# First, second and last RMS norm of a two-block transformer kernel: squares by parts, normalisation by halves or chunks, and a reciprocal in two halves

## Chip, cores and metric

The kernel runs on one core of one Trainium2 chip. The metric is the device time of one execution in microseconds. Of the kernel before, three runs were timed; one more execution was taken by the profiler.

## What is computed

Two blocks on x of 256 tokens by 2048 features, all float32. The rows that matter here:

```python
def rmsnorm(x, w):
    xf = x.astype(jnp.float32)
    xf = xf * lax.rsqrt(jnp.mean(xf * xf, axis=-1, keepdims=True) + EPS)
    return (xf * w.astype(jnp.float32)).astype(x.dtype)

# first_block
h = rmsnorm(x, ln1_w)                     # first norm
proj = h @ w_in                           # z, xbc, dt, q, k, v, f
y_ssd = ssd_group(...)                    # scan; its output is normalised in two groups of 512 features
y_fox = fox_group(...)                    # 16 heads of attention with a forget gate
x = x + jnp.concatenate([y_ssd, y_fox], axis=-1) @ w_out
x = x + peer(rmsnorm(x, ln2_w), ...)      # second norm, then 16384 experts
x = rmsnorm(x, lnf_w)

# second_block: conformer convolution and attention, cross attention, then
nm = rmsnorm_2(h, g_mlp[l])
h = h + jnp.square(jax.nn.relu(nm @ w1[l])) @ w2[l]
return rmsnorm_2(h, g_final)              # last norm
```

## The kernel before

**Weights as a stream.** All large weights lie in one stream of units of 128x2048 float32 (1 MB). SyncE loads them into four buffers (`raw`), and loads a buffer again when the unit in it has been split (`split_done`). Each unit is split into two float32r parts. ScalarE copies it (`hi`, tile w_hi), VectorE subtracts the copy from the original (`lo`, tile w_lo). `ahead(u)` on either engine does this for unit u+2 once TensorE has finished unit u (w_hi and w_lo have two buffers each). TensorE multiplies high by high, high by low and low by high: `feature_unit` does 48 matmuls of 256 columns for a unit, `row_unit` 24 of 512 columns.

**Tiles turned.** A matmul wants the activations with features on partitions. `turn_tile` transposes one of 16 feature tiles (two TensorE transposes) into one of four banks; ScalarE (`scaled_tile`) copies it with the norm's weight as scale into the high part of the tile a_both, VectorE (`scaled_lo`) computes the low part. TensorE may take a bank again when the low part of the tile four before it is written (`tmp_split`).

**Norms.** ScalarE's `square` squares a half of x (128 tokens by 2048) and sums into stat; GpSimd's `rsqrt` takes mean, epsilon and the power -0.5 (`rs_done`); VectorE's `normalise` multiplies both halves of x by it (`normed`). What stands around the three norms:

- First norm. ScalarE: two squares, casts of units 0 and 1, the high part of the small dt weights (wdtf to wd), 16 scaled tiles. VectorE: differences of units 0 and 1, `normalise`, the low part of wd, 16 low parts. TensorE: 16 tiles turned, 48 small matmuls for dt, their copy and two transposes, then 12 units of xbc. GpSimd issues the four small loads (consts, cols, rows, wdtf); all that need any of them wait for all of them (`s_small` 64).
- Second norm. The last out1 units end in `add_chunk`, in which VectorE adds 128x512 for each half of the tokens to x. After the last one come `squares`, the root, `normalise`, 16 tiles turned, and only then the first wq unit.
- Last norm. The same after the last down3 unit, with the norm's weight (`wide`) in VectorE's operation. SyncE then writes out each half of the tokens as it is ready (`fin`).

**The reciprocal.** In step 25 of 38 steps, in which v1, z, q, k and the first out1 units run beside the scan and the attention, VectorE takes the reciprocal of 128x512 root values (`rms`). Steps 25 to 28 scale two of eight tiles each with it and split them. Behind this stand in every step `head_max` (row maxima of one attention head's scores), `head_norm` of the head before, `out_split` in every second step, and `ahead`. TensorE may write the next head's scores only after `head_max` (one bank).

The order on each engine is the program's own, written out by hand; engines meet at semaphores only.

```python
if s == 25:
    eng.wait_ge(rt_done, 2)
    own.do(eng.reciprocal(rms[:, :, :], rms[:, :, :]))
if 25 <= s < 29:
    for i in (2 * (s - 25), 2 * (s - 25) + 1):
```

## Time and profile before

| what | us |
|---|---|
| median of three runs | 3184.81 |
| lowest, highest run | 3183.85, 3185.7 |
| profiled execution, device time | 3187.75 |
| its span, first to last instruction | 3185.9 |
| TensorE busy in the span | 3067.4 |
| VectorE busy | 2237.3 |
| ScalarE busy | 1400.6 |
| GpSimd busy | 143.3 |

The span is that of the profiled execution; the 1.85 us around it lie ahead of the first and behind the last instruction. Busy times of engines overlap. The mean granted clock of TensorE over the span is 0.989 of full speed (2.4 GHz; the lower level is 1.2 GHz).

### The profile page before, as it was taken

The numbers are of one execution on the slowest core, as the hardware profiler recorded it, in microseconds if no ns is written. First come the engines' busy times: TensorE is split into PE (matmuls) and PEld (weight loads), VectorE is DVE, ScalarE is ACT, GpSimd is POOL, SyncE is SP. The second block draws the span as 40 slices with busy tenths as digits, with TensorE's granted clock in tenths as the row PEclk, the third lists the DMA queues.
The fourth block names the chain that finished last, engine by engine and source line by source line (L and its number), as shares of the span: only waits on it lengthen the run. The fifth ranks groups of instructions, "written<-read, shape, count | busy, mean of one in ns | idle before, by whom it ended". The sixth has DMA issues, their size and how long they took to land.

```text
span 3185.9 us, 49641 instructions
## 1 busy us (share of the span) xinstructions
PE 3067.4 (96%) x19428; PEld 2810.2 (88%) x19428; DVE 2237.3 (70%) x3255; ACT 1400.6 (44%) x1640; POOL 143.3 (4%) x168
## 2 busy tenths in 40 slices
PE   6999989999999999999999999999898999999997
PEld 6898879899999999999999999998787888888886
DVE  4666548999867888888888677687655646555564
ACT  3465443356444444444444445334444333333332
POOL 1000000000101101010101000000000000000000
PEclk9999999999999999999999999999999999999999
DMA  4433454456767888888888664544343555555553
GB/s 186 178 141 131 146 197 148 170 189 235 244 245 279 314 300 311 298 310 300 308 298 312 239 238 172 186 166 152 130 174 107 197 190 189 188 188 194 186 188 126
DMA packets 95548, 673.14 MB, mean 211 GB/s; under 512 B 11528, under 2 KB 11552, under 8 KB 15424
## 3 DMA queue, kind: packets, MB, share of 16 engines
q1 hardware_dynamic: 77184, 562.07, 48.9%
q0 software_dynamic: 16224, 94.72, 8.8%
q10 hardware_dynamic: 2016, 14.68, 1.2%
q8 instruction: 80, 1.31, 0.2%
q14 instruction: 44, 0.36, 0.0%
HBM read 652.48 MB, written 18.89 MB: 211 GB/s over the span
## 4 chain that ended last, share of the span: by engine, by line
PE 85%; DVE 11%; ACT 2%; issue 1%; DMA 0%; DVEq 0%; SPq 0%; POOL 0%; POOLq 0%; ACTq 0%
PE bank L1768 29%; PE bank L1769 15%; PE bank L1796 6%; PE bank L1798 6%; PE bank L1797 6%; PE bank L1746 6%; PE bank L1748 5%; PE bank L1747 5%; DVE w_lo L1033 4%; PE bank L1774 2%; DVE pick_a L1429 1%; ACT w_hi L631 1%; DVE pick_b L1424 1%; PE bank L1860 1%; PE bank L1824 1%
## 5 line engine op out<-in xcount | busy, mean ns | idle before, releaser
L1033 DVE TENSOR_TENSOR w_lo<-raw,w_hi 128x2048 fp32r<-128x2048 f32 x532 | 1218.3, 2290 | 570.1 <-ACT w_hi L631 548.1
L1768 PE MATMUL bank<-a_both,w_hi 128*128 128x448 f32 (+1 forms) x3840 | 1258.3, 380 | 6.9 <-DVE a_both L1050 3.9
L1769 PE MATMUL bank<-a_both,w_lo 128*128 128x224 f32 (+1 forms) x4096 | 1060.5, 269 | 0.0
L1768 PEld LDWEIGHTS bank<-a_both,w_hi 128*128 128x128 f32 x3840 | 721.4, 188 | 90.3 <-DVE a_both L1050 4.4
L1769 PEld LDWEIGHTS bank<-a_both,w_lo 128*128 128x128 f32 x4096 | 778.2, 190 | 11.6
L631 ACT ACTIVATE w_hi<-raw 128x2048 fp32r<-128x2048 f32 x308 | 588.4, 1911 | 409.3 <-PE bank L1798 399.7
L1746 PE MATMUL bank<-a_both,w_hi 128*128 128x256 f32 (+1 forms) x1984 | 571.2, 288 | 19.3 <-DVE w_lo L1033 14.0
L644 ACT ACTIVATE w_hi<-raw 128x1536 fp32r<-128x1536 f32 x224 | 333.6, 1489 | 570.2 <-PE bank L1769 568.8
L1747 PE MATMUL bank<-a_both,w_hi 128*128 128x256 f32 (+1 forms) x1984 | 559.2, 282 | 0.0
L1748 PE MATMUL bank<-a_both,w_lo 128*128 128x256 f32 (+1 forms) x1984 | 559.1, 282 | 0.0
L1746 PEld LDWEIGHTS bank<-a_both,w_hi 128*128 128x128 f32 x1984 | 383.4, 193 | 26.9 <-issue 12.5
L1747 PEld LDWEIGHTS bank<-a_both,w_hi 128*128 128x128 f32 x1984 | 383.5, 193 | 0.3
L1748 PEld LDWEIGHTS bank<-a_both,w_lo 128*128 128x128 f32 x1984 | 383.1, 193 | 0.0
L1796 PE MATMUL bank<-w_hi,a_both 128*128 128x512 f32 x960 | 378.6, 394 | 4.3 <-DVE a_both L1677 3.4
L1798 PE MATMUL bank<-w_hi,a_both 128*128 128x512 f32 x960 | 375.8, 392 | 0.0
L1797 PE MATMUL bank<-w_lo,a_both 128*128 128x512 f32 x960 | 375.7, 391 | 0.0
L1796 PEld LDWEIGHTS bank<-w_hi,a_both 128*128 128x128 f32 x960 | 181.8, 189 | 43.1 <-issue 5.0
L1798 PEld LDWEIGHTS bank<-w_hi,a_both 128*128 128x128 f32 x960 | 181.5, 189 | 38.5
L1797 PEld LDWEIGHTS bank<-w_lo,a_both 128*128 128x128 f32 x960 | 181.6, 189 | 37.4
L1768 PE MATMUL bank<-e_both,w_hi 128*128 128x448 f32 x480 | 152.3, 374 | 0.0
L650 ACT ACTIVATE w_hi<-raw 128x512 fp32r<-128x512 f32 x224 | 138.3, 617 | 0.0
L1769 PE MATMUL bank<-e_both,w_lo 128*128 128x224 f32 x512 | 130.3, 265 | 0.0
(314 smaller groups left out, 2436.8 us busy)
## 6 DMA issues: line engine op xcount, KB each, us to landing
raw<-stream_dram SPq DMA_DIRECT2D x532, 1024.0 KB
gates_scratch<-stage ACTq DMA_DIRECT2D x14, 1024.0 KB, 4.8
gbuf<-gates_scratch POOLq DMA_DIRECT2D x30, 448.0 KB, 6.9
x<-x_dram SPq DMA_DIRECT2D x2, 1024.0 KB, 6.5
x_scratch<-x POOLq DMA_DIRECT2D x1, 2048.0 KB, 11.0
wide<-wide_dram POOLq DMA_DIRECT2D x2, 1024.0 KB, 9.0
mem<-mem_dram POOLq DMA_DIRECT2D x1, 2048.0 KB, 9.6
xm<-x_scratch POOLq DMA_DIRECT2D x1, 2048.0 KB, 9.0
```

What stands on the lines that cost most here:

```text
L631: eng.activation(w_hi[k % SPLIT][:, :], raw[:, k % RAW, :], ACT.Copy).then_inc(hi_done, 1)
L644: eng.activation(w_hi[k % SPLIT][:, 0:PART], raw[:, k % RAW, 0:PART], ACT.Copy)
L650: eng.activation(w_hi[k % SPLIT][:, PART:UNIT], raw[:, k % RAW, PART:UNIT], ACT.Copy).then_inc(hi_done, 1)
L1033: eng.tensor_tensor(w_lo[k % SPLIT][:, :], raw[:, k % RAW, :], w_hi[k % SPLIT][:, :].bitcast(F32), ALU.subtract).then_inc(split_done, 1)
L1746: mm(o, hi[:, ks], tile(0, kt), start=kt == 0, stop=False)
L1747: mm(o, hi[:, ks], tile(1, kt), start=False, stop=False)
L1748: last = mm(o, lo[:, ks], tile(0, kt), start=False, stop=kt == KT - 1)
L1768: mm(o, hi[:, ks], pair, start=kt == 0, stop=False)
L1769: inst = mm(o2, lo[:, ks], pair[:, 0, :], start=False, stop=False, skip_group_check=True)
L1796: mm(o, tile(0, k0 + k)[:, ts], hi[:, ns], start=first and k == 0, stop=False)
L1797: mm(o, tile(0, k0 + k)[:, ts], lo[:, ns], start=False, stop=False)
L1798: last = mm(o, tile(1, k0 + k)[:, ts], hi[:, ns], start=False, stop=end and k == 3)
```

## The change

**First norm.** GpSimd loads cols and consts first, under `s_small` (32), then wdtf and rows under a semaphore of their own, `s_dtf`. GpSimd takes the root of each half of the tokens as its square is ready (`rs_first`), and VectorE normalises that half. On ScalarE and VectorE the casts and differences of units 0 and 1 move behind the 16 turned tiles; ScalarE's copy of wdtf stands between the eighth and ninth of them, and VectorE's low part of it behind the sixteenth.

**Reciprocal.** Half of it in step 25, half in step 26; the scaling and splitting move from steps 25 to 28 to steps 27 to 30.

**Second norm.** ScalarE squares 128x512 at a time (`chunk_square`), three of four chunks beside units 8 to 14 of out1, the fourth after the last addition. VectorE sums the parts and takes mean and epsilon (`sum_squares`), GpSimd only the power. The first half of the tokens is normalised by VectorE, the second by ScalarE, both by chunks of 512 features. TensorE turns the first eight tiles ahead of the first wq unit, and the others inside it, behind its fourth and eighth tile. The cast and the difference for the next unit stand between chunks.

**Last norm.** Squares by chunks, as above. VectorE multiplies x by the norm's weight by chunks (`widen_final`), and multiplies by the root at the end: VectorE the first half of the tokens, ScalarE the second, each in two parts of 128x1024. Four output transfers take the place of two.

The diff, cut:

```diff
@@ SyncE
-            for tt in range(TT):
-                eng.wait_ge(fin, tt + 1)
-                eng.dma_start(out[tt * P:(tt + 1) * P, :], x[:, tt, :]).then_inc(s_out, 16)
-            eng.wait_ge(s_out, 32)
+            for half in range(2):
+                hs = slice(half * 1024, half * 1024 + 1024)
+                eng.wait_ge(fin, half + 1)
+                eng.dma_start(out[0:P, hs], x[:, 0, hs]).then_inc(s_out, 16)
+                eng.wait_ge(fin_act, half + 1)
+                eng.dma_start(out[P:T, hs], x[:, 1, hs]).then_inc(s_out, 16)
+            eng.wait_ge(s_out, 64)
@@ GpSimd
+            eng.dma_start(cols[:, :], cols_in).then_inc(s_small, 16)
             eng.dma_start(consts[:, :], consts_in).then_inc(s_small, 16)
-            eng.dma_start(cols[:, :], cols_in).then_inc(s_small, 16)
-            eng.dma_start(rows[:, :], rows_in.partition_broadcast(P)).then_inc(s_small, 16)
-            eng.dma_start(wdtf[:, :, :], wdtf_in).then_inc(s_small, 16)
+            eng.dma_start(wdtf[:, :, :], wdtf_in).then_inc(s_dtf, 16)
+            eng.dma_start(rows[:, :], rows_in.partition_broadcast(P)).then_inc(s_dtf, 16)
...
-            rsqrt("ln1")
+            for tt in range(TT):
+                eng.wait_ge(sq_done, tt + 1)
+                own.do(eng.tensor_scalar(stat[:, 4 + tt:5 + tt], stat[:, tt:tt + 1], 1.0 / D, EPS, ALU.mult, ALU.add))
+                eng.tensor_tensor(stat[:, 2 + tt:3 + tt], stat[:, 4 + tt:5 + tt], stat[:, 12 + tt:13 + tt], ALU.pow).then_inc(rs_first, 1)
...
-            rsqrt("ln2")
+            eng.wait_ge(lmean_done, 1)
+            eng.tensor_tensor(stat[:, 2:4], stat[:, 4:6], stat[:, 12:14], ALU.pow).then_inc(rs_done, 1)
@@ ScalarE
-            eng.wait_ge(resid, 2)
-            squares("ln2", x)
-            ahead(UNIT0["out1"] + 15)
-            scaled_tiles("ln2")
+                if j in (8, 9, 12):
+                    chunk_square(OUT1_FREE, lsq_done, {8: 0, 9: 1, 12: 2}[j])
+            chunk_square(OUT1_FREE, lsq_done, 3)
...
+            eng.wait_ge(rs_done, NQ["ln2"] + 1)
+            norm_chunk(0)
+            for c in range(4):
+                if c < 3:
+                    norm_chunk(c + 1)
+                scaled_chunk("ln2", c)
+                if c == 1:
+                    ahead(UNIT0["out1"] + 15)
...
+            chunk_square(DOWN_FREE, fsq_done, 3)
+            eng.wait_ge(rs_done, NQ["final"] + 1)
+            eng.wait_ge(y_final, 8)
+            for half in range(2):
+                hs = slice(half * 1024, half * 1024 + 1024)
+                eng.activation(x[:, 1, hs], x[:, 1, hs], ACT.Copy, scale=stat[:, 3:4]).then_inc(fin_act, 1)
@@ VectorE
-                if s == 25:
-                    eng.wait_ge(rt_done, 2)
-                    own.do(eng.reciprocal(rms[:, :, :], rms[:, :, :]))
-                if 25 <= s < 29:
-                    for i in (2 * (s - 25), 2 * (s - 25) + 1):
+                if s in (25, 26):
+                    eng.wait_ge(rt_done, s - 24)
+                    own.do(eng.reciprocal(rms[:, s - 25, :], rms[:, s - 25, :]))
+                if 27 <= s < 31:
+                    for i in (2 * (s - 27), 2 * (s - 27) + 1):
...
+            def norm_chunk(c):
+                cs = slice(c * 512, c * 512 + 512)
+                eng.tensor_scalar(norm[:, 0, cs], x[:, 0, cs], stat[:, 2:3], None, ALU.mult).then_inc(norm_dve, 1)
@@ TensorE
-            eng.wait_ge(normed, 4)
-            turn("ln2", norm)
+            norm_turn(0)
+            norm_turn(1)
...
-                    feature_unit(s, a1, "ln2" if s == 0 else None)
+                    feature_unit(s, a1, "ln2" if s == 0 else None, rest_turn if s == 0 else None)
```

How the instructions stand on VectorE at three places. w_lo is the difference of a weight unit, L1033 before and L1085 in the change; L1050 and L1102 are the low parts of turned tiles.

VectorE at the start of the program, before:

```order
L1033 TENSOR_TENSOR w_lo_52<-raw,w_hi_50 128x2048 [waits hi_done]
L1033 TENSOR_TENSOR w_lo_53<-raw,w_hi_51 128x2048 [waits hi_done]
L1118 TENSOR_SCALAR norm<-x,stat 128x2048 [waits rs_done]
L1118 TENSOR_SCALAR norm<-x,stat 128x2048
L1159 TENSOR_TENSOR wd_lo<-wdtf,wd_hi 128x512 [waits wd_done]
L1050 SCALAR_TENSOR_TENSOR a_both<-bank,cols,a_both 128x256 [waits tmp_full] x16
```

and in the change:

```order
L1209 TENSOR_SCALAR norm<-x,stat 128x2048 [waits rs_first] x2
L1102 SCALAR_TENSOR_TENSOR a_both<-bank,cols,a_both 128x256 [waits tmp_full,s_small]
L1102 SCALAR_TENSOR_TENSOR a_both<-bank,cols,a_both 128x256 [waits tmp_full] x15
L1213 TENSOR_TENSOR wd_lo<-wdtf,wd_hi 128x512 [waits wd_done]
L1085 TENSOR_TENSOR w_lo_52<-raw,w_hi_50 128x2048 [waits hi_done]
L1085 TENSOR_TENSOR w_lo_53<-raw,w_hi_51 128x2048 [waits hi_done]
```

The two differences and wd_lo moved from ahead of the turned tiles to behind them.

VectorE at the second norm, before (stat is written by `resid_ready`):

```order
L1106 MEMSET stat 128x1 [waits dve_own]
L1118 TENSOR_SCALAR norm<-x,stat 128x2048 [waits rs_done]
L1118 TENSOR_SCALAR norm<-x,stat 128x2048
L1050 SCALAR_TENSOR_TENSOR a_both<-bank,cols,a_both 128x256 [waits tmp_full] x16
L1033 TENSOR_TENSOR w_lo_53<-raw,w_hi_51 128x2048 [waits hi_done]
```

and in the change:

```order
L1373 TENSOR_REDUCE stat<-psq 128x2 [waits lsq_done]
L1374 TENSOR_SCALAR stat<-stat 128x2 [waits dve_own]
L1380 TENSOR_SCALAR norm<-x,stat 128x512 [waits rs_done]
L1380 TENSOR_SCALAR norm<-x,stat 128x512
L1102 SCALAR_TENSOR_TENSOR a_both<-bank,cols,a_both 128x256 [waits tmp_full] x4
L1380 TENSOR_SCALAR norm<-x,stat 128x512
L1102 SCALAR_TENSOR_TENSOR a_both<-bank,cols,a_both 128x256 [waits tmp_full] x4
L1380 TENSOR_SCALAR norm<-x,stat 128x512
L1102 SCALAR_TENSOR_TENSOR a_both<-bank,cols,a_both 128x256 [waits tmp_full] x4
L1085 TENSOR_TENSOR w_lo_53<-raw,w_hi_51 128x2048 [waits hi_done]
L1102 SCALAR_TENSOR_TENSOR a_both<-bank,cols,a_both 128x256 [waits tmp_full] x4
```

The unit's difference, which stood behind all sixteen tiles, now stands ahead of the last four.

VectorE in step 25, before (rms holds the roots, inT the scan's output, fox_p and amax belong to head_max):

```order
L1033 TENSOR_TENSOR w_lo_52<-raw,w_hi_50 128x2048 [waits hi_done]
L1289 RECIPROCAL rms<-rms 128x512 [waits rt_done]
L1292 SCALAR_TENSOR_TENSOR inT<-inT,cols,rms 128x256 [waits dve_own]
L1043 CAST a_both<-inT 128x256 [waits dve_own]
L1044 TENSOR_TENSOR a_both<-inT,a_both 128x256 [waits dve_own]
L1292 SCALAR_TENSOR_TENSOR inT<-inT,cols,rms 128x256
L1043 CAST a_both<-inT 128x256 [waits dve_own]
L1044 TENSOR_TENSOR a_both<-inT,a_both 128x256 [waits dve_own]
L1130 ISA fox_p,amax<-bank,consts 128x128 [waits at_t,at_s]
```

and in the change:

```order
L1085 TENSOR_TENSOR w_lo_52<-raw,w_hi_50 128x2048 [waits hi_done]
L1345 RECIPROCAL rms<-rms 128x256 [waits rt_done]
L1182 ISA fox_p,amax<-bank,consts 128x128 [waits at_t,at_s,dve_own]
L1182 ISA amax 128x1
L1182 ISA fox_p,amax<-bank,consts 128x256
```

Between the unit's difference and head_max one half of the reciprocal stands where the whole and six more operations stood.

## Rows read from the trace of the kernel before

**Rows 1.** Stretches: busy us of PE, PEld, DVE, ACT, POOL; clock; DMA share, GB/s.

```profile
32.83:40.85 8.02, 7.55 (x50) 6.34 (x51) 0.00 (x0) 0.37 (x1) 0.00 (x0) 0.79 0.00 0
441.45:457.55 16.10, 6.84 (x34) 4.78 (x33) 9.38 (x19) 11.94 (x20) 3.56 (x4) 0.68 0.61 211
...
295.60:299.60 4.00, 3.96 (x14) 2.65 (x15) 3.90 (x6) 1.45 (x5) 0.96 (x2) 0.57 0.01 1
3169.95:3185.90 15.95, 0.00 (x0) 0.00 (x0) 6.08 (x6) 4.00 (x4) 0.89 (x2) 0.61 0.32 131
```

**Rows 2.** Time line at the start: start us, us, engine, line, operation [idle before <-releaser].

```profile
1.98 0.56 POOL L510 DMA_DIRECT2D cols<-cols_dram  x1
...
11.29 0.19 ACT L686 ACTIVATION_READ_ACCUMULATOR junk_early<-x 128x1 f32 x1
...
19.77 0.61 ACT L736 ACTIVATE wd_hi<-wdtf 128x512 fp32r<-128x512 f32 x1
...
24.50 0.68 DVE L1159 TENSOR_TENSOR wd_lo<-wdtf,wd_hi 128x512 fp32r<-128x512 f32 x1
...
25.43 6.79 ACT L696 ACTIVATE a_both<-bank,cols 128x256 fp32r<-128x256 f32 x16 [5.04 <-PE bank L1824]
25.93 6.84 DVE L1050 SCALAR_TENSOR_TENSOR a_both<-bank,cols,a_both 128x256 fp32r<-128x256 f32 x16 [0.75 <-ACT a_both L696]
...
32.83 0.47 PE L1872 MATMUL bank<-a_both,wd_hi 128*32 128x256 f32 x2 [1.13 <-DVE a_both L1050]
```

**Rows 3.** DMA issues up to 45 us: what, KB, us from issue to landing.

```profile
wdtf<-wdtf_dram POOLq DMA_DIRECT2D x1, 256.0 KB, 13.6
cols<-cols_dram POOLq DMA_DIRECT2D x1, 222.0 KB, 10.2
```

**Rows 4.** Time line around the reciprocal, and a reciprocal of 128x256 elsewhere.

```profile
288.94 3.35 DVE L1289 RECIPROCAL rms<-rms 128x512 f32<-128x512 f32 x1
...
294.70 0.28 DVE L1130 CUSTOM_DVE_ANT_0 fox_p<-bank,consts 128x128 f32<-128x128 f32 x1
...
295.64 0.53 PE L1948 MATMUL bank<-qk_pad 128*128 128x128 f32 x2 [3.96 <-issue]
...
313.49 0.46 PE L1948 MATMUL bank<-qk_pad 128*128 128x128 f32 x2 [0.58 <-issue]
...
2297.58 1.75 DVE L1671 RECIPROCAL ln_buf<-ln_buf 128x256 f32<-128x256 f32 x1
```

**Rows 5.** Time line at the second norm, by engine.

```profile
441.53 1.29 DVE L1083 TENSOR_TENSOR x<-bank,x 128x512 f32<-128x512 f32 x2 [1.20 <-PE bank L1798]
...
448.22 2.48 DVE L1118 TENSOR_SCALAR norm<-x,stat 128x2048 f32<-128x2048 f32 x2 [5.18 <-POOL stat L520]
...
458.78 2.28 DVE L1033 TENSOR_TENSOR w_lo<-raw,w_hi 128x2048 fp32r<-128x2048 f32 x1
...
447.47 0.71 POOL L520 TENSOR_TENSOR stat<-stat 128x2 f32<-128x2 f32 x1
...
451.48 6.83 ACT L696 ACTIVATE a_both<-bank,cols 128x256 fp32r<-128x256 f32 x16 [2.43 <-PE bank L1824]
463.58 0.38 ACT L826 ACTIVATE qT<-bank 128x256 f32<-128x256 f32 x1 [5.27 <-PE bank L1748]
```

**Rows 6.** Single operations elsewhere in the trace: ns of one, min/median/max.

```profile
L902 ACT ACTIVATE junk_part<-xm x16: 630/632/633, 1905.7 to 1959.6; 128x512 f32<-128x512 f32 x16
...
L1545 DVE TENSOR_TENSOR xm<-xm,wide_l x8: 683/684/693, 1911.4 to 1958.8; 128x512 f32<-128x512 f32 x8
```

**Rows 7.** Time line of the last units and behind the last matmul.

```profile
3159.07 1.92 ACT L631 ACTIVATE w_hi<-raw 128x2048 fp32r<-128x2048 f32 x1 [3.52 <-PE bank L1798]
...
3169.95 1.41 DVE L1085 SCALAR_TENSOR_TENSOR x<-bank,stat,x 128x512 f32<-128x512 f32 x2 [6.64 <-PE bank L1798]
...
3176.75 4.61 DVE L1115 SCALAR_TENSOR_TENSOR x<-x,stat,wide 128x2048 f32<-128x2048 f32 x2 [5.17 <-POOL stat L520]
3179.13 2.61 SPq L501 DMA_DIRECT2D out_dram<-x  x2
```

More of the change, by code:

```diff
@@ L391, in build @@
         NQ = {n: i for i, n in enumerate(NORMS)}
+        SQ = {n: i for i, n in enumerate(n for n in NORMS if n not in ("ln2", "final"))}
+        OUT1_FREE, DOWN_FREE = 4 * ROUND0["out1"] + 4, 4 * ROUND0[f"down{FF_ROUNDS - 1}"] + 4
         BUILDS = ["ln1", "ln2"] + [f"u{r}" for r in range(2, PEER_ROUNDS)] + ["gmem", "gmix", "gcross", "gmlp"]
@@ L1019, in _ @@
             feature(f"up{FF_ROUNDS - 1}", 16, 0, half(None, BQ[f"up{FF_ROUNDS - 1}"]))
-            row_units(f"down{FF_ROUNDS - 1}", 2, last=True)
-            eng.wait_ge(resid, 12)
-            squares("final", x)
+            u0 = UNIT0[f"down{FF_ROUNDS - 1}"]
+            for j in range(14):
+                ahead(u0 + j)
+                if j in (8, 9, 12):
+                    chunk_square(DOWN_FREE, fsq_done, {8: 0, 9: 1, 12: 2}[j])
+            chunk_square(DOWN_FREE, fsq_done, 3)
[4 more added lines that the diff above has]
+                eng.activation(x[:, 1, hs], x[:, 1, hs], ACT.Copy, scale=stat[:, 3:4]).then_inc(fin_act, 1)
         @block.vector
@@ L1312, in _, with sum_squares, norm_chunk @@
             resid_ready()
-            normalise("ln2", x, norm)
-            scaled_los("ln2")
-            ahead(UNIT0["out1"] + 15)
+            def sum_squares(done, out):
+                eng.wait_ge(done, 4 * TT)
+                own.do(eng.tensor_reduce(stat[:, 0:2], psq[:, 0, :, :], AX.X, ALU.add))
+                eng.tensor_scalar(stat[:, 4:6], stat[:, 0:2], 1.0 / D, EPS, ALU.mult, ALU.add).then_inc(out, 1)
+            sum_squares(lsq_done, lmean_done)
+            def norm_chunk(c):
+                cs = slice(c * 512, c * 512 + 512)
+                eng.tensor_scalar(norm[:, 0, cs], x[:, 0, cs], stat[:, 2:3], None, ALU.mult).then_inc(norm_dve, 1)
+            eng.wait_ge(rs_done, NQ["ln2"] + 1)
+            norm_chunk(0)
+            norm_chunk(1)
+            for c in range(4):
+                scaled_lo_chunk("ln2", c)
+                if c < 2:
+                    norm_chunk(c + 2)
+                if c == 2:
+                    ahead(UNIT0["out1"] + 15)
             def best8(k, jobs):
```

87 lines of the change are left out of this document (71 added, 16 removed).

## The prediction

> **What bounds the kernel now.** I read the page's busy times first, then granted clock and busy time by stretch, then the time lines around the four edited places. TensorE is busy for 3067.4 of 3185.9 us. An edit on VectorE or ScalarE is therefore worth only what it takes out of TensorE's idle or slow time, or out of the stretches ahead of its first and behind its last matmul. Four such stretches are touched. (1) At the start TensorE's first transpose runs only once VectorE has normalised x, which ends near 24.5, and the dt matmuls begin at 32.83 [rows 2]. (2) Around the full reciprocal TensorE idles 3.96 us and then runs slowly [rows 1, 4]. (3) At the second norm 16.10 us lie between the last out1 matmul and the first wq matmul, and they hold only the transposes [rows 1, 5]. (4) After the last matmul nothing is left but the add, the norm and the output [rows 7].
>
> **First norm.** The squares stay. ScalarE ends the second one at 11.29 + 0.19 = 11.48 [rows 2]. Now each half has its own root. The nearest row for GpSimd is 0.71 us for the root of two columns [rows 5]; with the small scalar step and the handovers ahead of it I take 1.0 us from square to root, so 12.5 for the second half. The weight casts no longer stand ahead, so VectorE does its half in 1.24 us (2.48 for two [rows 5]): first half while x's second tile is being squared, second half 12.5 to 13.8. Transposes start at 13.85 instead of 24.7. Their constants must have landed: cols and consts together take the place of consts and cols, and the later of them was issued at 1.98 [rows 2] and landed 10.2 us later, at 12.2 [rows 3]. That is earlier than 13.85, by 1.6 us. The sixteen turns are a chain in which ScalarE (6.79) and VectorE (6.84) both work without a gap, one tile apart [rows 2]; it takes the same 8.1 us. Into it comes ScalarE's cast of wdtf, 0.61 us [rows 2], which nothing hides as VectorE follows one tile behind (0 if the ring of four banks absorbs it). Behind it stands VectorE's wd_lo, 0.68 us [rows 2], which used to lie under the first transposes and now is on the path. The dt matmuls start at 13.85 + 8.1 + 0.6 + 0.7 = 23.3, against 32.83: **9.5 us** saved. The casts of the first two units now run behind the turns. ScalarE ends its turns near 22 and both casts near 26, VectorE's two differences of 2.28 us [rows 5] end near 28.6; the dt block's 8.02 us [rows 1] lasts until 31.3, and this is what hides them. Without that cover their end would cost up to 4 us. A stream buffer is refilled once its difference is done. That was before VectorE normalised (24.50 - 2.48 = 22.0) and is now at 26 to 28.6, some 7 us later; the data is wanted only four units of about 5.8 us later (463.58 less 457.55, with a handover [rows 1, 5]). What cannot be read is the clock: the dt block had a mean granted clock of 0.79, so some 3.4 of its 8.02 us ran at the 1.2 GHz level and cost 1.7 us [rows 1]. With none of it slow the gain is 11.2, with twice as much 7.8. These are the bounds. Everything up to the reciprocal follows in the same order and merely comes earlier.
>
> **Reciprocal.** One of 128x512 takes 3.35 us, and three more operations twice over stand behind it, so that head_max starts at 294.70 and TensorE's next scores 0.94 us later, at 295.64 [rows 4]. The halves should take 1.75 us each, as the row of a 128x256 reciprocal elsewhere shows [rows 4]. In step 25 head_max then starts at 288.94 + 1.75 = 290.7 and the scores may start at 291.6, just ahead of TensorE's arrival at 291.7 (295.64 less 3.96). The idle 3.96 us go. So does the slow spell that followed them: mean clock 0.57 over 4.00 us is 3.4 us at 1.2 GHz, worth 1.7 us [rows 1]. In step 26 the second half of 1.75 us stands where scaling stood. One step's scaling took VectorE from 292.3 (288.94 + 3.35) to 294.70, 2.4 us, more than a half of the reciprocal; it moves to steps 27 to 30. Before, steps 25 and 26 were covered by the long stall, and of the other two with scaling one stalled TensorE, for 0.58 us [rows 4]. As a stall also gives VectorE time for the following step, I expect one in every two steps: two in steps 27 to 30 instead of one. Gain 3.96 + 1.7 - 0.6 = **5.1 us** (3.4 if the slow spell falls elsewhere, 5.7 if no second stall).
>
> **Second norm.** Three of four chunks are squared under the out1 units. What remains after the last addition (second tile done at 441.53 + 1.29 = 442.8 [rows 5]) is one chunk: its first tile overlaps the second addition, its second costs 0.63 [rows 6] and 0.19 for the sum's read [rows 2], until 443.75. Then VectorE's reduction and scalar step, two small operations like that read, with handovers 0.45, then the root 0.71 [rows 5] with handovers 0.85: rs_done at 445.05, against 448.22 [rows 5]. Normalising goes by chunks: VectorE a quarter of 1.24 us, ScalarE about 0.6 us (its 128x512 square takes 0.63 [rows 6]). Transposes start at 445.7, ScalarE's first turn at 446.4 against 451.48 [rows 5]. But ScalarE now does more: four normalised chunks of 0.55 (two before the first turn), 16 turns in 6.83, and in their middle the cast for the next unit (1.92 [rows 7], of which 1.85 count in a row of operations). It ends at 446.4 + 6.8 + 1.1 + 1.85 = 456.2. VectorE has its difference for that unit ahead of the last four tiles: third chunk done 455.0, difference 455.0 to 457.2 (2.28 [rows 5]), last four tiles to 458.95. TensorE works on the unit as chunks come and has its last 12 matmuls left, 1.4 us: unit 0 ends at 460.4, where before it ended at 463.4 (ScalarE takes its result at 463.58 [rows 5]). **2.9 us** saved. At the 1.2 GHz level the last 12 matmuls cost 1.4 us more, 1.5 saved; if the difference were not on the path 4.3. The mean granted clock of this stretch was 0.68 before [rows 1]; a shorter idle time can hardly make that worse.
>
> **Last norm.** From the last addition (3169.95 + 1.41 = 3171.36) the old path has two squares (ScalarE busy for 4.00 us [rows 1]), the root, and 4.61 us for two halves of x, with the output issued at 3179.13 for the first [rows 7]. Now: last square done at 3172.2, reduction and scalar step 3172.65, root by 3173.5. VectorE multiplies the last chunk by the weights at the same time, two of 0.684 us [rows 6], done 3173.9, and that ends last. Then half a tile on VectorE, 0.64 (half of 1.24 [rows 5]): first output at 3174.6. ScalarE's halves (128x1024, between 0.63 for 512 [rows 6] and 1.92 for 2048: 1.05) are done at 3175.0 and 3175.95. Before, the first issue stood 6.8 us ahead of the span's end, which is the time of 2 MB and one latency. By that 3174.6 + 6.8 = 3181.4, against 3185.9: **4.5 us** (3.5 if four transfers cost 1 us more than two, 5.0 if root and weights overlap better). The squares and weights of the earlier chunks lie in idle time: a down3 unit lasts 1.92 + 3.52 = 5.4 us [rows 7], which leaves ScalarE 3.5 and VectorE, with 2.3 busy, 3.1; a pair of either takes 1.4 to 1.6 us.
>
> **A rule against it.** The trace of before has no GpSimd root beside a VectorE operation with two operands in SBUF: in rows 7 VectorE waits. The Trainium skill, SBUF — State Buffer, section Who interferes with whom, says that such a VectorE instruction and a GpSimd one that reads SBUF block each other for a whole instruction. No row here shows it. As a mechanism of this kernel: the root waits out the first weight multiplication and the second waits out the root, so the end comes by one root later, 0.7 us [rows 5].
>
> **Sum.** 9.5 + 5.1 + 2.9 + 4.5 = 22.0 us. The profiled execution took 3187.75 with a span of 3185.9, 1.85 around it; the sum would make it 3165.75. It is 2.9 us over the median of 3184.81 (0.1%), and the edits act alike in both, so the forecast is 3184.81 - 22.0 = 3162.8. All low ends together give 16.2 us and 3168.6, all high ends 26.2 and 3158.6.
>
> **Rivals.** (A) The second norm gains nothing: ScalarE's four added chunks and the cast between them put back what the earlier root gives, and the last matmuls run at the 1.2 GHz level. For it speaks that VectorE's difference stands ahead of the last chunk; against it that TensorE already works on early chunks. 3165.7. (B) A transfer sets the start: if consts lands only when all four small loads do (wdtf, two places behind cols, landed 13.6 us after its own issue, near 16.7 [rows 3]) transposes start 2.9 us later, 3165.7. ScalarE also waits for wdtf in the middle of the turns, but gets there at 17.9. (C) The port conflict, 3163.5. (D) Slower: fed in pieces from 13.85 on, TensorE stays at 1.2 GHz into the xbc units. Each microsecond so spent loses half; the 22.0 us are gone after 44 us, and with 70 us (twelve units of 5.8) the time is 3184.8 - 22 + 35 = 3198. Against it stands that the clock was back within the dt block [rows 1]. (E) The reciprocal's stall only moves to steps 27 to 30, 0.6 us in each of four: 3164.6 with the slow spell gone, 3166.3 with it kept.
>
> **How the numbers follow.** Chances: forecast 0.60, C 0.13, A 0.11, E 0.08, B 0.05, D 0.01, and 0.02 for a gain nearly all given back later by other slow-clock spells. Forecast, C, A, E and B lie between 3158.5 and 3168.5, which also holds the bounds of the terms; that is the range. Within 0.2% of before (about what a measurement of this kernel can tell from no change) means above 3178.4: 0.02, slower 0.01, with one more part for same from what I did not think of. Faster 0.96.
>
> **What would show it.** Right: dt matmuls near 23 and xbc near 31; no idle before the scores of step 26 and about 0.5 us in two of steps 27 to 30; wq unit 0 ending some 3 us nearer to the last out1 matmul; span ending about 11.5 us after the last addition starts (15.95 before [rows 1]). Wrong: a wait for cols or consts, a slow clock reaching into xbc, the last four tiles later than 16 us after the last addition, or an output transfer that starts late. The forecast fails as a whole if the stream of weights starves TensorE once it starts earlier.

## The result, and the profile after

The changed kernel takes 3163.14 us (median of 4 runs, 3160.92 to 3165.17) against 3184.62 for the kernel before beside it: ratio 0.9932, 95% interval 0.9915 to 0.9949. Two later sets gave 3163.47 (0.9933, 0.9916 to 0.9949) and 3163.00 (0.9928, 0.9915 to 0.9942). The forecast was 3162.8 us, faster by 22.0; the 13 executions of the three sets have their median at 3163.0, faster by 21.6. The profiled execution took 3165.17 with a span of 3163.4.

I locate the gain by the starts of VectorE's 532 weight differences, which both kernels compute in the same order (L1033 before, L1085 after): the shift of the same difference, taken between two places, is what the part between them gained. The last norm is read from the start of the last addition to the end of the span; "everything else" is what is left of the difference of the spans.

| part, us | forecast | profile after | eleven further profiles of it and its variants |
|---|---|---|---|
| first norm | 9.5 | 8.60 | 8.5 to 11.5 where unedited |
| reciprocal | 5.1 | 4.76 | 4.71 to 4.80 |
| second norm | 2.9 | 1.66 | 1.65 or 3.12 to 3.15 where unedited |
| last norm | 4.5 | 4.34 | 4.33 to 4.36 where unedited |
| everything else | 0 | 3.21 | -1.4 to 4.1 |

**First norm.** The time line at the start (start us, us, engine, line, operation, idle time before it and what ended it) answers to [rows 2]:

```profile
8.73 1.29 DVE L1209 TENSOR_SCALAR norm<-x,stat 128x2048 f32<-128x2048 f32 x1 [8.73 <-POOL stat L547]
...
12.35 1.29 DVE L1209 TENSOR_SCALAR norm<-x,stat 128x2048 f32<-128x2048 f32 x1 [2.34 <-POOL stat L547]
...
13.79 5.40 PE L1918 MATMUL bank<-consts,norm 128*128 128x128 f32 x24 [13.79 <-DVE norm L1209]
...
18.06 0.62 ACT L759 ACTIVATE wd_hi<-wdtf 128x512 fp32r<-128x512 f32 x1
...
22.22 0.68 DVE L1213 TENSOR_TENSOR wd_lo<-wdtf,wd_hi 128x512 fp32r<-128x512 f32 x1
...
23.05 0.60 PE L1966 MATMUL bank<-a_both,wd_hi 128*32 128x256 f32 x2 [1.82 <-DVE wd_lo L1213]
...
32.25 0.36 PE L1840 MATMUL bank<-a_both,w_hi 128*128 128x256 f32 x1
```

Turns began at 13.79 (forecast 13.85) and wd_lo stood last ahead of the dt matmuls, which began at 23.05 (forecast 23.3, 32.83 before). VectorE's normalisation was what released the turns, not a transfer. From the first dt matmul to the first xbc matmul at 32.25 (forecast near 31) it took 9.20 us, against the 8.02 us of [rows 1]. By stretches, the first of which holds the 48 dt matmuls alone (start:end us, busy us of PE, PEld, DVE, ACT and POOL, granted clock, DMA share, GB/s):

```profile
23.05:31.47 8.42, 8.42 (x48) 6.81 (x48) 4.49 (x2) 2.29 (x2) 0.00 (x0) 0.64 0.48 176
...
3151.72:3163.37 11.65, 0.00 (x0) 0.00 (x0) 4.35 (x8) 3.63 (x6) 1.07 (x1) 0.67 0.45 180
```

The mean clock was 0.64, so 2 x 0.36 x 8.42 = 6.1 us at the 1.2 GHz level, where [rows 1] had 3.4.

**Reciprocal.** In step 25 one half takes 1.75 us as forecast, and the scores of step 26 at 283.07 follow without the idle time of 3.96 us of [rows 4]. Two stalls of 0.58 us show, ahead of the scores of steps 28 (299.32) and 30 (315.58). The first stands in the kernel before too, at 313.49 [rows 4]; the second is new:

```profile
280.34 1.75 DVE L1345 RECIPROCAL rms<-rms 128x256 f32<-128x256 f32 x1
282.12 0.29 DVE L1182 CUSTOM_DVE_ANT_0 fox_p<-bank,consts 128x128 f32<-128x128 f32 x1
...
283.07 0.46 PE L2042 MATMUL bank<-qk_pad 128*128 128x128 f32 x2
...
299.32 0.46 PE L2042 MATMUL bank<-qk_pad 128*128 128x128 f32 x2 [0.58 <-issue]
...
315.58 0.46 PE L2042 MATMUL bank<-qk_pad 128*128 128x128 f32 x2 [0.58 <-issue]
```

**Second norm.** The time line from the last addition on, which starts at 428.18 here and at 441.53 in [rows 5]:

```profile
428.18 1.29 DVE L1135 TENSOR_TENSOR x<-bank,x 128x512 f32<-128x512 f32 x2 [1.20 <-PE bank L1892]
...
430.86 0.71 POOL L564 TENSOR_TENSOR stat<-stat 128x2 f32<-128x2 f32 x1 [145.64 <-DVE stat L1374]
...
431.67 1.33 ACT L850 ACTIVATE norm<-x,stat 128x512 f32<-128x512 f32 x2 [1.29 <-POOL stat L564]
...
433.23 1.75 ACT L718 ACTIVATE a_both<-bank,cols 128x256 fp32r<-128x256 f32 x4 [0.23 <-PE bank L1918]
...
441.44 2.28 DVE L1085 TENSOR_TENSOR w_lo<-raw,w_hi 128x2048 fp32r<-128x2048 f32 x1
443.63 1.65 DVE L1102 SCALAR_TENSOR_TENSOR a_both<-bank,cols,a_both 128x256 fp32r<-128x256 f32 x4
...
445.34 0.49 PE L1840 MATMUL bank<-a_both,w_hi 128*128 128x256 f32 x1 [1.91 <-DVE a_both L1102]
448.21 0.38 ACT L870 ACTIVATE qT<-bank 128x256 f32<-128x256 f32 x1 [5.25 <-PE bank L1842]
```

TensorE waits 1.91 us for VectorE's last four tiles and then needs 2.87 us (445.34 to 448.21) for its last 12 matmuls, which take 1.74 us in another execution (after_again, below): they ran at 1.2 GHz.

**Last norm.** Behind the last matmul, as in [rows 7]:

```profile
3151.72 1.41 DVE L1137 SCALAR_TENSOR_TENSOR x<-bank,stat,x 128x512 f32<-128x512 f32 x2 [5.39 <-PE bank L1892]
...
3154.29 1.29 DVE L1806 TENSOR_TENSOR x<-x,wide 128x512 f32<-128x512 f32 x2
3154.47 1.07 POOL L643 TENSOR_TENSOR stat<-stat 128x2 f32<-128x2 f32 x1 [705.36 <-DVE stat L1374]
3155.65 1.42 DVE L1822 TENSOR_SCALAR x<-x,stat 128x1024 f32<-128x1024 f32 x2
3155.69 2.19 ACT L1074 ACTIVATE x<-x,stat 128x1024 f32<-128x1024 f32 x2 [1.71 <-DVE x L1806]
3156.43 0.35 SPq L514 DMA_DIRECT2D out_dram<-x  x1
```

GpSimd's root took 1.07 us, not 0.71 as at L564, while it ran beside VectorE's multiplication. It ended at 3155.54, the multiplications at 3155.58.

### The profile page after: what moved, and what is told of

Its sections match the earlier page's. It is cut to its first block, busy times and chain, and to the rows that moved or that the text cites. A ratio compares the mean times of both kernels' runs of the same rounds, so it can differ in the third digit from the quotient of the medians.

```text
span 3163.4 us, 49697 instructions
## 1 busy us (share of the span) xinstructions
PE 3065.3 (97%) x19428; PEld 2810.0 (89%) x19428; DVE 2239.1 (71%) x3268; ACT 1407.0 (44%) x1670; POOL 142.6 (5%) x168
## 4 chain that ended last, share of the span: by engine, by line
PE 86%; DVE 10%; ACT 3%; issue 1%; DMA 0%; ACTq 0%; POOL 0%; DVEq 0%; SPq 0%
PE bank L1862 29%; PE bank L1863 15%; PE bank L1890 6%; PE bank L1892 6%; PE bank L1891 6%; PE bank L1840 6%; PE bank L1842 5%; PE bank L1841 5%; DVE w_lo L1085 4%; PE bank L1868 2%; ACT w_hi L653 1%; DVE pick_a L1502 1%; PE bank L1954 1%; PE bank L2154 1%; DVE tmp L1269 1%
## 5 line engine op out<-in xcount | busy, mean ns | idle before, releaser
L1085 DVE TENSOR_TENSOR w_lo<-raw,w_hi 128x2048 fp32r<-128x2048 f32 x532 | 1218.4, 2290 | 543.3 <-ACT w_hi L653 521.0
```

What stands on the lines that cost most here:

```text
L1085: eng.tensor_tensor(w_lo[k % SPLIT][:, :], raw[:, k % RAW, :], w_hi[k % SPLIT][:, :].bitcast(F32), ALU.subtract).then_inc(split_done, 1)
```

## Experiments

### Does the program differ, or the execution?

**after_again**: the changed kernel, unchanged.

> The changed kernel once more, for what differs between two executions of one program. In the first profile of it the edits gave 8.6 (first norm), 4.75 (reciprocal), 1.65 (second norm) and 4.4 us (last norm), 19.4 together, and 3.1 us came from places that the change does not touch, where spells of the 1.2 GHz level stood in other places than before. Theory 1 (those 3.1 us belong to the execution, not to the program): the local gains repeat within 0.1 us, the slow spells outside the edited places stand elsewhere, and the span differs by up to 3 us. Rival (the shift of all work by 15 us causes them): spells and span repeat within 0.5 us.

Measured: first norm 9.83, reciprocal 4.71, second norm 3.12, last 4.34, and everything else -0.66 us, where the first profile had 8.60, 4.76, 1.66, 4.34 and +3.21. The sum is 21.3 us in one, 22.6 in the other. The reciprocal and the last norm repeat within 0.05 us; the first and the second norm do not, against what I expected. Stretches of this kernel, then of the same program in its third set (after_timed):

```profile
20.00:36.00 16.00, 13.71 (x98) 11.82 (x98) 11.83 (x19) 7.66 (x12) 4.71 (x5) 0.89 0.43 167
...
970.00:990.00 20.00, 18.22 (x117) 17.09 (x116) 18.09 (x23) 10.01 (x15) 6.51 (x3) 1.00 0.80 294
...
2235.00:2300.00 65.00, 55.90 (x219) 45.73 (x220) 36.67 (x61) 27.02 (x37) 0.00 (x0) 0.87 0.35 127
```

```profile
20.00:36.00 16.00, 13.71 (x111) 12.34 (x110) 13.17 (x27) 8.07 (x14) 5.67 (x6) 1.00 0.45 176
```

and of the first profile of the changed kernel:

```profile
20.00:36.00 16.00, 13.71 (x88) 11.43 (x88) 10.65 (x16) 7.62 (x12) 3.53 (x4) 0.79 0.42 164
...
970.00:990.00 20.00, 18.23 (x105) 17.00 (x105) 16.41 (x20) 8.46 (x14) 6.50 (x3) 0.91 0.76 295
...
2235.00:2300.00 65.00, 55.56 (x230) 45.41 (x229) 39.32 (x67) 27.25 (x37) 0.00 (x0) 0.92 0.38 130
```

One program, three executions: in 20 to 36 us the clock is 0.79, 0.89 and 1.00, and the first norm's gain 8.60, 9.83 and 11.26 us. At 970 one execution has a slow spell that the other lacks, and from 2235 on it is the other way round. Seen over nine profiles in which the first norm is as in the change, the gain is 8.54 to 8.87 us at a clock of 0.79, 9.45 to 9.83 at 0.89, and 11.06 to 11.49 at 1.00. The prediction's bounds for this term were 7.8 and 11.2; two of the nine profiles lie above them (11.26 and 11.49).

**before_again**: the kernel before, unchanged.

> The kernel before, unchanged, profiled again. Theory 1: the spells at the lower clock in stretches of light work belong to the execution, in kernel before as in the changed one. Then some of the 13 spells are at other places or of other lengths, and the span differs from 3185.93 by up to 3 us. Those that follow an idle stretch of TensorE of several us (behind the reciprocal near 295.9, the second norm near 446, the first norm near 33, the last norm) are expected at the same places again. Rival: the spells are all tied to places in the program; then all 13 come back within 1 us of their places, and the 3.1 us that the changed kernel gained in places which it did not edit would need a cause in the change.

Measured: span 3185.94 us, the same as the first profile to 0.01 us, by other pieces: first norm 1.87 us shorter, reciprocal 0.92 longer, second norm 0.27 shorter, the rest 1.21 longer. First the rows of this profile, then those of the first profile of before for the same stretches:

```profile
30.00:44.00 14.00, 12.40 (x100) 10.95 (x99) 6.93 (x17) 4.22 (x11) 4.73 (x5) 1.00 0.00 1
286.00:305.00 19.00, 15.04 (x98) 13.43 (x96) 14.58 (x33) 5.03 (x11) 0.96 (x2) 0.82 0.32 111
...
2250.00:2315.00 65.00, 55.56 (x218) 45.07 (x217) 38.86 (x67) 26.06 (x36) 0.00 (x0) 0.87 0.36 128
```

```profile
30.00:44.00 14.00, 12.38 (x85) 10.29 (x85) 5.44 (x14) 4.37 (x11) 2.92 (x4) 0.88 0.00 1
286.00:305.00 19.00, 15.04 (x107) 13.52 (x106) 15.73 (x33) 6.21 (x14) 0.96 (x2) 0.91 0.30 111
...
2250.00:2315.00 65.00, 55.56 (x218) 45.18 (x217) 39.01 (x67) 26.07 (x36) 0.00 (x0) 0.87 0.35 127
```

Both theories hold in part. Up to 600 us the spells moved or changed length: the one in the dt block, which I had expected to come back, is gone. From 790 us on, all came back at their places. So which places get a spell, and how long it lasts, differs between executions in part; the time in one place is uncertain by some 2 us although the total may agree. All gains by part in this document are read against the first profile of before. Read against before_again, the first norm would gain 1.87 us less, the reciprocal 0.92 more (5.7) and the second norm 0.27 less.

### Reciprocal

**recip_undone**: the reciprocal's order put back in the changed kernel.

```diff
-                if s in (25, 26):
-                    eng.wait_ge(rt_done, s - 24)
-                    own.do(eng.reciprocal(rms[:, s - 25, :], rms[:, s - 25, :]))
-                if 27 <= s < 31:
-                    for i in (2 * (s - 27), 2 * (s - 27) + 1):
+                if s == 25:
+                    eng.wait_ge(rt_done, 2)
+                    own.do(eng.reciprocal(rms[:, :, :], rms[:, :, :]))
+                if 25 <= s < 29:
+                    for i in (2 * (s - 25), 2 * (s - 25) + 1):
```

> The changed kernel with the reciprocal put back: one of 128 x 512 values at step 25 and the eight scaled tiles from step 25 on. The changed kernel gained 4.71 to 4.76 us in this part in five profiles. Theory: 3.96 us of it is TensorE's idle stretch, which comes back at its full length here, and the rest is the spell at the lower clock behind it (1.7 us) less the two stalls of 0.58 us at steps 27 and 30; so this part's gain falls to 0 +- 0.2 us, and a spell of 3.4 us at the lower clock shows up within 1 us of the idle stretch's end again, since this spell followed the idle time in the kernel before. Rival: the spell there belonged to that one execution, as the spells elsewhere do; then it is absent, and the part shows a gain of 1.5 to 1.7 us with the reciprocal undone.

Its time line at the scores of step 26:

```profile
277.88 3.34 DVE L1345 RECIPROCAL rms<-rms 128x512 f32<-128x512 f32 x1
...
284.57 0.77 PE L2042 MATMUL bank<-qk_pad 128*128 128x128 f32 x2 [3.96 <-issue]
```

The idle time is back to the hundredth, two matmuls take 0.77 us instead of 0.46 (the lower clock sets in at once), and the part's gain falls from 4.7 to 0.11 us. In both profiles of before and in this one a slow spell goes with this stall (in before_again it begins already within it and is longer); in no profile with the split reciprocal is there one. So this spell belongs to the stall. The gain is 3.96 us of idle time and 1.6 of slow clock less 0.8, the price of the added stall ahead of step 30's scores: in the first profile after the shift grows by 5.56 us (from 8.60 to 14.16) over steps 25 and 26 and falls back by 0.80 at that stall.

### Second norm

**ln2_lo_last**: VectorE splits the last four tiles ahead of the next unit's difference.

```diff
                 scaled_lo_chunk("ln2", c)
                 if c < 2:
                     norm_chunk(c + 2)
-                if c == 2:
+                if c == 3:
                     ahead(UNIT0["out1"] + 15)
```

> Second norm: VectorE's difference of the next weight unit stands behind the last four turned tiles, no longer ahead of them. Theory (the difference is on the path, and the idle time that it makes on TensorE ahead of its last 12 matmuls lets the clock fall): the last 12 matmuls start near 2.2 us earlier relative to the last addition, the idle 1.91 us nearly go, the slow spell at that place goes, and unit 0 of wq ends 2.0 to 3.5 us earlier. Rival (ScalarE's longer work is what ends last there, with four normalised chunks and the cast): VectorE only waits for ScalarE, and unit 0 ends less than 1 us earlier.

Unit 0's result and what comes next:

```profile
440.17 2.29 DVE L1085 TENSOR_TENSOR w_lo<-raw,w_hi 128x2048 fp32r<-128x2048 f32 x1
442.06 0.38 ACT L870 ACTIVATE qT<-bank 128x256 f32<-128x256 f32 x1 [2.38 <-PE bank L1842]
...
442.51 0.39 PE L1840 MATMUL bank<-a_both,w_hi 128*128 128x256 f32 x1 [0.48 <-DVE w_lo L1085]
```

The 1.91 us of waiting are gone; unit 1 now waits 0.48 us for the difference. Unit 0's result comes 16.74 us behind the start of the last addition, against 18.92 in after_again, 2.18 us earlier as the theory had it; the wait ahead of unit 1 takes some of it back. The part gains 4.56 us, 1.44 more than in after_again (3.12), so the difference was on the path, as the prediction had it, and could leave it.

**ln2_both**: besides, ScalarE casts the next unit's weights ahead of the root, not in the middle of the turns.

```diff
+            ahead(UNIT0["out1"] + 15)
             eng.wait_ge(rs_done, NQ["ln2"] + 1)
             norm_chunk(0)
             for c in range(4):
                 if c < 3:
                     norm_chunk(c + 1)
                 scaled_chunk("ln2", c)
-                if c == 1:
-                    ahead(UNIT0["out1"] + 15)
```

> As ln2_lo_last, and ScalarE's cast of the next weight unit stands ahead of its wait for the root, where ScalarE was idle for 1.29 us, and no longer between the second and third four tiles. Theory: the first normalised chunk is 0.5 us later, all behind the second four tiles 1.2 us earlier, and unit 0 of wq ends about 1 us earlier than in ln2_lo_last (3 to 4.5 us earlier than in the changed kernel). Rival (TensorE's own work at the 1.2 GHz level sets the pace once both are out of the way): no gain over ln2_lo_last.

```profile
430.16 1.91 ACT L653 ACTIVATE w_hi<-raw 128x2048 fp32r<-128x2048 f32 x1
...
431.98 1.32 ACT L850 ACTIVATE norm<-x,stat 128x512 f32<-128x512 f32 x2
...
439.08 1.57 ACT L718 ACTIVATE a_both<-bank,cols 128x256 fp32r<-128x256 f32 x4 [1.13 <-PE bank L1917]
```

The first chunk starts 4.05 us behind the addition's start instead of 3.49 (the cast delays it), and later ScalarE waits for TensorE's turns, 1.13 us here and 0.74 at the next chunk. Unit 0's result comes 17.4 us behind the addition; in the four profiles with the edit of ln2_lo_last alone (two of them also with that of wd_early) it comes after 16.5 to 17.1. So the theory, 1 us earlier, is wrong, and the rival's outcome, no gain over ln2_lo_last, came true: the part gains 3.86 us, against 4.15 to 4.82 in those four. The rival's reason is half shown: TensorE ran at 1.2 GHz from 431.4 to 438.2, ahead of the first wait, but at full clock ahead of the second. The cast costs nothing where the change has it: it fills time in which ScalarE would wait for TensorE.

### First norm

**wd_early**: dt's weights are cast and split ahead of the turned tiles, and the vectors have a semaphore of their own.

```diff
...
             eng.wait_ge(s_small, 32)
-            for kt in range(8):
-                scaled_tile("ln1", kt)
-            eng.wait_ge(s_dtf, 32)
+            eng.wait_ge(s_dtf, 16)
             eng.activation(wd[0][:, :, :], wdtf[:, :, :], ACT.Copy).then_inc(wd_done, 1)
-            for kt in range(8, KT):
+            for kt in range(KT):
                 scaled_tile("ln1", kt)
...
             eng.wait_ge(s_small, 32)
-            scaled_los("ln1")
             eng.wait_ge(wd_done, 1)
             eng.tensor_tensor(wd[1][:, :, :], wdtf[:, :, :], wd[0][:, :, :].bitcast(F32), ALU.subtract).then_inc(wd_done, 1)
+            scaled_los("ln1")
```

> First norm: ScalarE's copy of wdtf and VectorE's low part of it stand ahead of the turned tiles instead of in their middle and behind them, and wdtf has a semaphore of its own so that rows is not waited for. Theory (both are on the path, 0.6 and 0.7 us, and the gap that they make is a part of why the dt block runs slow): wdtf lands at 13.8, the copy takes ScalarE's idle time up to 14.55, the dt matmuls start 1.0 to 1.3 us earlier, and if the slow spell shrinks by one half xbc starts 2.7 us earlier, else 1.0 to 1.3. Rival (wdtf lands too late): the turns start later by what it is late, and xbc starts no earlier than at 32.25.

```profile
14.31 7.20 PE L1917 MATMUL bank<-consts,norm 128*128 128x128 f32 x32 [14.31 <-DVE norm L1208]
14.42 0.63 ACT L758 ACTIVATE wd_hi<-wdtf 128x512 fp32r<-128x512 f32 x1 [2.50 <-DMA wdtf<-wdtf_dram]
```

Measured: the first norm gains 10.17 us at a clock of 0.89, against 9.83 and 9.45 for the change at that clock, so 0.3 to 0.7 us more; the dt matmuls start at 22.64, where the nine profiles without the edit have 22.86 to 23.41. That is below the 1.0 to 1.3 us that I expected. The turns began 0.5 us later here than in the first profile (14.31 for 13.79) because x landed later in this execution, and from there to the dt matmuls it took 8.33 us instead of 9.26. But wdtf lands only near 14.3 (2.51 + 11.8), and its copy cannot start earlier. In lo_wd and lo_wd_again, where the turns begin at 13.89 and 13.99, the copy (14.48 and 14.37) does hold up the first tiles: there the way from the turns to the dt matmuls takes 9.07 and 8.65 us, which is 0.2 and 0.6 less than 9.26. So the rival, wdtf lands too late, is true in part.

### Last norm: the rival of the shared port

**tail_apart**: the last chunk is multiplied only after the root.

```diff
             sum_squares(fsq_done, fmean_done)
+            eng.wait_ge(rs_done, NQ["final"] + 1)
             widen_final(3)
             eng.wait_ge(y_final, 8)
-            eng.wait_ge(rs_done, NQ["final"] + 1)
```

> The changed kernel, with one edit in its last norm: VectorE waits for GpSimd's root before it multiplies the last column chunk with the weights, so that the two no longer run beside each other. Rival C of the prediction (the two engines share access to the SBUF): the root takes 0.71 us again as before the change, where it took 1.07; then the pair of 1.29 us follows, and the scaling starts at about 3154.3 + 0.9 + 1.4 = 3156.6 instead of 3155.65, 0.9 to 1.0 us later. If the root's 1.07 us is not from VectorE's work beside it, it stays 1.07 and the scaling starts 1.3 us later. In both cases the local gain of the last norm falls from 4.34 to about 3.0 to 3.4 us.

```profile
3151.39 1.41 DVE L1137 SCALAR_TENSOR_TENSOR x<-bank,stat,x 128x512 f32<-128x512 f32 x2 [5.39 <-PE bank L1892]
...
3154.14 0.71 POOL L643 TENSOR_TENSOR stat<-stat 128x2 f32<-128x2 f32 x1 [705.14 <-DVE stat L1374]
3154.88 1.29 DVE L1806 TENSOR_TENSOR x<-x,wide 128x512 f32<-128x512 f32 x2 [0.83 <-POOL stat L643]
3156.21 1.42 DVE L1822 TENSOR_SCALAR x<-x,stat 128x1024 f32<-128x1024 f32 x2
```

The root takes 0.71 us again. So its 1.07 us come from the work beside it: the conflict of rival C exists. Its price is 0.36 us on GpSimd; VectorE's pair takes 1.29 us beside the root and without it. By the Trainium skill (SBUF — State Buffer, Who interferes with whom) a VectorE instruction with two SBUF inputs contends with a GpSimd instruction that reads SBUF, for ports that are an exclusive lock. The runs show a wait of GpSimd and none of VectorE. In the first profile after, the root starts 0.18 us into the first multiplication of 0.68; had it waited that one out before doing anything, it would have lost 0.50 us and not 0.36. Where in the root's 0.71 us the wait falls, no run shows. Scaling starts 4.82 us behind the addition instead of 3.93: keeping the engines apart costs 0.89 us.

**tail_early**: one half of the last chunk is multiplied ahead of the reduction.

```diff
+            widen_final(3, (0,))
             sum_squares(fsq_done, fmean_done)
-            widen_final(3)
+            widen_final(3, (1,))
```

> The changed kernel, with one edit in its last norm: VectorE's multiplication of the last column chunk with the norm's weights is taken apart by token halves; the first half is multiplied as soon as its own square is read (beside ScalarE's second square), ahead of the reduction, and only the second half stands beside GpSimd's root. Theory 3: what ends last ahead of the scaling is VectorE's pair of multiplications (3154.29 to 3155.58 in the changed kernel), and GpSimd's root of 1.07 us ends with it, so the root's length costs nothing as long as the pair stands there; with one multiplication gone the root becomes the last. If the root is long because VectorE's two-input multiplication runs beside it, and for that operation alone, it will be about 0.9 to 1.1 us here and the scaling starts 0.1 to 0.3 us earlier; if its length has another reason it stays 1.07 us at any place. Rival: the root falls to 0.71 us (half of the cover gone), and the scaling starts 0.45 us earlier. Elsewhere nothing changes: reciprocal -4.7, second norm -3.1 or -1.7 us (by whether a spell at the lower clock falls on it).

```profile
3152.62 1.41 DVE L1137 SCALAR_TENSOR_TENSOR x<-bank,stat,x 128x512 f32<-128x512 f32 x2 [5.39 <-PE bank L1893]
...
3155.19 0.68 DVE L1806 TENSOR_TENSOR x<-x,wide 128x512 f32<-128x512 f32 x1
3155.37 1.07 POOL L643 TENSOR_TENSOR stat<-stat 128x2 f32<-128x2 f32 x1 [705.36 <-DVE stat L1374]
3156.53 2.19 ACT L1074 ACTIVATE x<-x,stat 128x1024 f32<-128x1024 f32 x2 [1.64 <-POOL stat L643]
```

The root is 1.07 us long beside one multiplication as beside two, and now ends last (releaser POOL). VectorE's scaling starts 3.93 us behind the addition, as in the changed kernel, and ScalarE's 3.91 against 3.97: nothing gained that shows, less than the 0.1 to 0.3 I expected. VectorE's pair and the lengthened root are two paths of the same length.

### A kernel that beats both

**after_timed**, **lo_timed** (the edit of ln2_lo_last) and **lo_wd** (that and the edit of wd_early), timed together; then **lo_wd_again**.

> The changed kernel, timed again as the mark for the two kernels beside it. Expected ratio to the kernel before 0.9932 within 0.0010, median 3163 to 3164 us. In its profile: first norm's gain 8.6 to 8.9 us if 6.8 us at the lower clock stand between the turns and the first dt matmuls, 9.5 to 10.2 if 3.4 us, 11.1 to 11.5 if none; reciprocal 4.7; second norm 3.1, or 1.7 if a spell falls on its last 12 matmuls; last norm 4.34.

> The changed kernel with the one edit of ln2_lo_last: in the second norm VectorE splits the last four turned tiles before it computes the low half of slot 15's weights, no longer after. ln2_lo_last gained 4.56 us in this part where the changed kernel gained 3.12 or 1.66. Theory 2 (a TensorE that waited 1.91 us for VectorE with 12 matmuls left): 1.4 us less than the changed kernel in the median, and up to 2.9 against executions with the spell, so 3160.5 to 3162.2 us, ratio 0.9924 to 0.9929. Rival: it is taken back later, since the spells at the lower clock in the parts that follow come in two patterns some 3 to 4 us apart, and the median falls on the other pattern; then the median is 3163 us again and only the local shift shows a gain.

> Both edits together (second norm as in lo_timed; in the first norm the weights of dt are cast and split as soon as they land, as in wd_early). Expected another 0.3 us less than lo_timed from the first norm, which is below what the medians can tell apart: 3160.2 to 3162.0 us. If the vectors that come last on their queue set the start of what follows, it is the same as lo_timed or up to 0.5 us longer.

> lo_wd once more, unchanged. Its first five executions had a median of 3159.03 us, 4.0 us below the changed kernel timed beside it, while lo_timed, which differs from it by the weights of dt alone, came out at 3163.96. Local shifts can carry 1.0 to 1.4 us of that (second norm) and 0.3 us (first norm). If the rest is chance of where the spells at the lower clock fall, the median now comes out near 3161.5 us. If the edit of the dt weights also keeps spells away (TensorE's idle time ahead of the dt matmuls is 1.08 us there, 1.82 in the changed kernel), 3159 repeats, and the profile's first norm shows 0 or 3.4 us at the lower clock rather than 6.8.

| kernel | median us | executions | ratio to before |
|---|---|---|---|
| after_timed | 3163.00 | 3162.22 to 3164.58 | 0.9928 (0.9915 to 0.9942) |
| lo_timed | 3163.96 | 3160.64 to 3165.54 | 0.9932 (0.9918 to 0.9945) |
| lo_wd | 3159.03 | 3155.87 to 3162.78 | 0.9917 (0.9903 to 0.9930) |
| lo_wd_again | 3158.37 | 3156.32 to 3165.17 | 0.9922 (0.9909 to 0.9936) |

lo_timed gained 4.15 us in the second norm, 1.0 more than after_timed, and was not faster in the median (3160.5 to 3162.2 expected): the time came out as the rival had it. Why its slower executions lost it, no kept trace shows. lo_wd was faster both times. Its ten executions have their median at 3158.7, the changed kernel's 13 at 3163.0: 4.3 us, 0.14%, and eight of the ten lie below the lowest of the 13, though the intervals against before overlap. The second norm of these two profiles gains 4.25 and 4.82 us, 1.1 and 1.7 more than the change without a spell on its last matmuls, and the first norm 11.44 and 11.79, up to 0.7 more than the change at full clock. The rest goes with less time at the lower clock; this is the first norm of lo_wd_again:

```profile
20.00:36.00 16.00, 14.40 (x116) 12.95 (x116) 12.74 (x26) 8.73 (x15) 5.68 (x6) 1.00 0.43 163
```

Eight of the ten executions of lo_wd have a mean clock of 0.992 or 0.993 over the span (seven of them 0.993), of the changed kernel's 13 one has 0.993 and the others 0.991 or 0.992. Both profiles of lo_wd have the full clock in the first norm; of the nine with the order of the change three have. Whether the shorter wait ahead of the dt matmuls (1.1 us instead of 1.8) keeps the spell away is not settled: wd_early, with the same edit, had one.

## Why the prediction was right, and where it was not

**The time.** 3162.8 forecast, 3163.14 measured. Part of that closeness is chance: the first profile's four edited parts sum to 19.4 us and unedited places give another 3.2, while the profile of after_timed, whose span is 0.6 us shorter, has 23.5 in the edited parts and -0.3 elsewhere. No run takes back the edits of the first or of the last norm as a whole; their gains are read from time lines, and what each single edit in them is worth is not shown.

**First norm, 9.5.** Each step up to the dt matmuls was within 0.3 us: turns at 13.79 for 13.85, wd_lo on the path, the casts of the first units hidden behind the dt block, dt at 23.05 for 23.3. ScalarE's cast of wdtf was put at 0.6 us of path; from the turns to VectorE's last tile it took 8.5 us instead of 8.0, so it cost some 0.5. What failed in the first profile is the assumption that the block keeps 3.4 us at the lower clock: there were 6.1 in it, it took 9.20 us instead of 8.02, and xbc came at 32.25 for 31. By the stretch from 20 to 36 us other profiles had between 0 and 6.7 us. At the clock assumed, the gain is 9.45 to 9.83.

**Reciprocal, 5.1.** The term for the later stalls was 0.6 and came out at 0.8; the lower clock behind the stall was worth 1.6 and not 1.7 (5.56 less 3.96). Two stalls among the scores of steps 27 to 30, where one had been, is what the prediction named. Measured 4.7 to 4.8 in every profile with the edit, against the first profile of before. Rival E, the stall moving to each of four steps, is out; recip_undone shows that the slow spell goes with the stall.

**Second norm, 2.9.** The chain was right in its members. Counted from the last addition's start: ScalarE's first turn at 5.05 us for 4.9, VectorE's difference at 13.26 for 13.5, last four tiles begun at 15.45, not later than the 16 us named as a sign of being wrong, and done at 17.10 for 17.4; ScalarE's normalised chunk took 0.67 us for 0.55. The unit's result was to come at about 19, and came at 18.92 in after_again; the part gained 3.12 to 3.15 there and in three more profiles. The first profile had 1.66 since its last 12 matmuls took 2.87 us instead of 1.74, and the next unit lost 0.35 more at the lower clock; the low bound named for just that, 1.5, fits. Rival A, nothing gained, is out.

**Last norm, 4.5.** First output 4.71 us behind the addition's start for 4.65, end of the span 11.65 for 11.45. Four output transfers instead of two cost nothing near the 1 us of the low bound.

**Rival C.** The mechanism was there (root 1.07 for 0.71), and its price on the path was nothing that shows (VectorE's pair still ended last, by 0.04 us), for 0.7 predicted: I had let VectorE's second multiplication wait for the root, which no run shows. **Rival B** is out: cols and consts had landed by 12.4 (1.96 + 10.4), ahead of VectorE's norm. **Rival D**, the slower case, is out: the longest spell at the lower clock near the start ended ahead of the xbc units at 32.25.

**What the prediction left out** is that unedited parts vary by -1.4 to +4.1 us between profiles. I gave 0.02 to "given back later". All 13 executions of the changed kernel (3160.45 to 3166.41) lie within the range all the same; in its three profiles the edited parts had least (19.4) where the rest had most (3.2). Whether one makes up for the other as a rule, three profiles do not show.

## What to carry to other kernels

Where one engine is busy for 96% of the span, price an edit only by that engine's idle time around it, and by the slow clock that follows such idle time: the idle 3.96 us here were worth 5.6. A term that depends on the clock should be forecast with the clock's range, and an edit of 1 to 2 us should be judged by a local shift in several profiles of both kernels, since one profile's place can be 2 us off by where the slow spells fell. Before moving work away from another engine's, see whether its delay is on the path: the root that was lengthened by half cost nothing, and keeping it apart cost 0.89 us.

## What the runs showed of the hardware

- The same program has slow spells at partly different places from one execution to the next (20 to 36 us: 0.79, 0.89, 1.00), with spans only 0.01 us apart for before and 1.8 apart for the changed kernel.
- A wait of 3.96 us of TensorE went with the 1.2 GHz level, which set in during the wait or within 0.3 us of its end, in all three profiles that have it; a wait of 1.91 us (the second norm's last tiles) was followed by it in three profiles of seven.
- A GpSimd operation on 128x2 values takes 0.71 us alone and 1.07 beside VectorE's 128x512 multiplication of two SBUF operands, one or two of them alike; VectorE's took 1.29 for two, beside the root and without it.
